# Two transformer blocks in one kernel: joining steps of the third attention

## The reference

```
# 8 heads of 64 in 2 key groups; 512 queries
kc, vc = compress(k_c), compress(v_c)            # 31 compressed keys
s_c = q . kc * scale;  p_c = softmax(s_c masked) * valid_c
o_c = p_c . vc
s_s = q . k_blocks[selected]                     # 8 of at most 8 blocks of 64: all past keys
o_s = softmax(s_s masked) . v_blocks
s_w = q . k_band                                 # a causal window of 256 keys
o_w = softmax(s_w masked) . v_band
g = sigmoid(g_logit)                             # three gates per head
o = g[0] * o_c + g[1] * o_s + g[2] * o_w
```

## Time and profile before

| what | value |
|---|---|
| median of 3 runs | 2524.85 us (2523.75 to 2526.11) |
| the profiled execution | 2522.84 us, its span 2521.0 us |
| granted TensorE clock in it | 1.00 |
| PE, DVE, ACT busy in the span | 99%, 55%, 37% |
| third attention, first scores to the next stage's first product | 1964.16 to 2090.23 us |

### The profile page before, as it was taken

The page is one execution under the profiler, slowest core; times in us unless marked ns, Lnnn a source line. Parts: engine busy times, 40 slices in busy tenths (PEclk is TensorE's granted clock), DMA queues, the critical chain, the costliest instruction groups (busy, mean ns, idle before and its releaser), DMA issues.

```text
span 2521.0 us, 30069 instructions
## 1 busy us (share of the span) xinstructions
PE 2501.9 (99%) x11841; PEld 2023.9 (80%) x11841; DVE 1395.2 (55%) x1962; ACT 943.7 (37%) x1379; POOL 60.4 (2%) x77
## 2 busy tenths in 40 slices
PE   9999999999999999999999999999999999999999
PEld 7788888888888877888888888888777658888887
DVE  6556366645556655555663444566654676733433
ACT  5432334322334444223442232445544574422222
POOL 6000000000000000000001000000000001000000
PEclk9999999999999999999999999999999999999999
DMA  4222223444443311222343333222222111222222
GB/s 164 67 84 96 88 101 104 150 147 150 150 136 115 104 68 69 99 101 84 109 139 126 134 115 133 95 91 101 101 93 75 51 34 67 101 100 100 94 90 100
DMA packets 38629, 260.04 MB, mean 103 GB/s; under 512 B 4417, under 2 KB 4673, under 8 KB 8049
## 3 DMA queue, kind: packets, MB, share of 16 engines
q1 hardware_dynamic: 32976, 226.92, 26.2%
q10 hardware_dynamic: 5296, 30.20, 3.4%
q0 software_dynamic: 240, 1.28, 0.2%
HBM read 256.29 MB, written 2.10 MB: 102 GB/s over the span
## 4 chain that ended last, share of the span: by engine, by line
PE 94%; DVE 4%; ACT 1%; issue 1%; DMA 0%; SPq 0%; DVEq 0%; ACTq 0%
PE ps L2010 65%; PE ps L2037 9%; PE ps L2241 6%; PE ps L2063 5%; PE ps L2184 2%; PE ps L2225 2%; PE ps L2205 1%; PE ps L2467 1%; DVE w_lo L1139 1%; PE ps L2483 1%; PE ps L2163 0%; DVE a_lo L1263 0%; PE ps L2523 0%; PE ps L2329 0%; DVE T L1258 0%
## 5 line engine op out<-in xcount | busy, mean ns | idle before, releaser
L1139 DVE TENSOR_TENSOR w_lo<-raw,w_hi 128x2048 fp32r<-128x2048 f32 x208 | 477.5, 2295 | 325.1 <-ACT w_hi L570 275.3
L2010 PE MATMUL ps<-a_hi,w_hi 128*128 128x512 f32 x1408 | 550.4, 391 | 0.5 <-DVE w_lo L1139 0.3
L2010 PE MATMUL ps<-a_hi,w_lo 128*128 128x512 f32 x1408 | 547.9, 389 | 0.0
L2010 PE MATMUL ps<-a_lo,w_hi 128*128 128x512 f32 x1408 | 547.8, 389 | 0.0
L570 ACT ACTIVATE w_hi<-raw 128x2048 fp32r<-128x2048 f32 x198 | 376.4, 1901 | 404.0 <-PE ps L2010 338.2
L2010 PEld LDWEIGHTS ps<-a_hi,w_hi 128*128 128x128 f32 x1408 | 264.3, 188 | 57.2 <-issue 1.1
L2010 PEld LDWEIGHTS ps<-a_lo,w_hi 128*128 128x128 f32 x1408 | 264.4, 188 | 55.4 <-issue 1.0
L2010 PEld LDWEIGHTS ps<-a_hi,w_lo 128*128 128x128 f32 x1408 | 264.3, 188 | 54.8
L2010 PE MATMUL ps<-f_hi,w_hi 128*128 128x512 f32 x708 | 275.4, 389 | 0.0
L2010 PE MATMUL ps<-f_lo,w_hi 128*128 128x512 f32 x708 | 275.4, 389 | 0.0
L2010 PE MATMUL ps<-f_hi,w_lo 128*128 128x512 f32 x708 | 275.4, 389 | 0.0
(11 more groups left out here) (384 smaller groups left out, 3559.8 us busy)
## 6 DMA issues: line engine op xcount, KB each, us to landing
raw<-weights SPq DMA_DIRECT2D x209, 1024.0 KB, 4.9
ada_w<-ada ACTq DMA_DIRECT2D x24, 1024.0 KB, 4.9
merged<-cmp_w SPq DMA_DIRECT2D x2, 1024.0 KB, 5.8
out<-h SPq DMA_DIRECT2D x8, 256.0 KB, 2.0
h<-x_t SPq DMA_DIRECT2D x3, 512.0 KB, 7.1
raw<-weights SPq DMA_DIRECT2D x4, 256.0 KB, 5.1
kt<-c_row ACTq DMA_DIRECT2D x2, 512.0 KB, 3.6
pads<-p_t ACTq DMA_DIRECT2D x2, 512.0 KB, 4.0
```

The lines of the kernel that those rows point to most:

```text
L1139: dve.tensor_tensor(w_lo[n % 2][:, w], raw[n % 2][:, w], w_hi[n % 2][:, w].bitcast(F32), ALU.subtract)\
L2010: ins = pe.matmul(dst, a[i], b[j], start=done == 0, stop=done == total - 1)
```

## The change

1. In query blocks 0 and 1 the selected and the window step become one step with `parts=2`: one score matmul per head over both key sets (the key operand `kt[r, 0:2, 0:w]` has two stretches), one mask addition and one maximum for four rows of sums, four exponentials, four weighings, and one list of value products. The list has 28 steps instead of 36.
2. A compressed step is done for both heads at once: three DVE instructions before the exponential, one exponential, four DVE instructions after it.
3. PE's value products wait in a list `due` and are issued for two steps at a time (alone at the end of a tile, if they are due there). The transposed probabilities get a third pair of buffers (`qx`), and ACT's copies wait for the products of step s-3 instead of s-2.
4. The maxima, sums and scales of this attention get columns of their own in `small`, which grows from 28 to 60.
5. The table that deals out the 48 gate pieces is a new one.

The lists of the first two kinds of attention and all other stages are as before.

```diff
@@ nsa_steps
+                    if b < 2:
+                        out.append(dict(
+                            w=2 * w, parts=2, masks=((w - P, C("causal")),),
+                            gate=[gt[:, b, 3 * hd + 1:3 * hd + 3] for hd in heads],
+                            sets=[(qt[r, t, b * P:(b + 1) * P], kt[r, 0:2, 0:w]) for r in half],
+                            values=[selected[g] + window[g] for g in range(2)],
...
@@ pieces
-                share = [0] + [2, 2, 1, 1, 2, 1, 1, 1, 1] * 3 + [2, 2, 2, 2, 1, 1, 1, 1]
+                share = [0] + [3, 2, 2, 1, 1, 1, 2] * 3 + [3, 3, 2, 2, 1, 1]
@@ buffers of the transposed probabilities
+            return (pT[0], pT[1], T[2], T[3], qx[:, 2, :], qx[:, 3, :])[2 * (s % 3) + j]
+        def kept(which):
+            return 3 if which > DEPTH else 2
@@ ACT
+                    if x["kind"] == "cmp":
+                        act.activation(both_probs(s), both_scores(s)[:, :, 0:P], ACT.Exp).then_inc(sem("exp_done"), 2)
+                        return
+                    n, w = parts(x)
                     for j in range(2):
+                        m = 2 * s + j
+                        for a in range(n):
+                            at, k, t = slice(a * w, (a + 1) * w), maximum_at(which, s) + n * j + a, total_at(which, s) + n * j + a
+                            ins = act.activation(probs(which, m)[:, at], score_bank(m)[:, at], ACT.Exp,
+                                                 bias=small[:, k:k + 1], scale=1.0, accum_out=small[:, t:t + 1])
+                        ins.then_inc(sem("exp_done"), 1)
...
@@ DVE, maxes
+                        both, top = both_scores(s)[:, :, 0:P], small[:, 52:60].rearrange("p (j b) -> p j b", j=2)
+                        seq(dve.tensor_tensor(both, both, C("cmp_mask").unsqueeze(1).to_broadcast([P, 2, P]), ALU.add))
+                        both = both_blocks(both)
+                        seq(dve.tensor_reduce(top, both, AX.X, ALU.max))
...
+                    if parts(x)[0] == 2:
+                        both = both[:, :, 0:w].rearrange("p j (a n) -> p j a n", a=2)
+                        (lo, mask), = x["masks"]
+                        seq(dve.tensor_tensor(both[:, :, :, lo:lo + P], both[:, :, :, lo:lo + P],
+                                              mask.unsqueeze(1).unsqueeze(1).to_broadcast([P, 2, 2, P]), ALU.add))
+                        dve.tensor_reduce(small[:, k:k + 4].rearrange("p (j a) -> p j a", j=2), both, AX.X, ALU.max,
+                                          negate=True).then_inc(sem("max_made"), 1)
+                        return
...
@@ PE, attention
-                    if s >= 1:
-                        apply(s - 1)
-                apply(len(steps) - 1)
+                    if s >= 1 and steps[s - 1]["kind"] != "cmp":
+                        due.append(s - 1)
+                    if len(due) == 2 or due and (not ahead or steps[due[0]]["closes"]):
+                        for i in due:
+                            apply(i)
+                        due = []
+                for i in due + [len(steps) - 1]:
+                    apply(i)
```

More of the change, by code:

```diff
@@ L321, in nsa_steps @@
                     n = w - k0 * P
[L322 to L337, removed]
+                    base = dict(out=[ps[7][r, b * P:(b + 1) * P] for r in half], tile=t, kind="pair", first=False)
@@ new lines, in nsa_steps @@
+                    selected = [[vt[:, j, 64 * g:64 * g + 64] for j in range(b + 1)] for g in range(2)]
+                    window = [[vt[:, j, P + 64 * g:P + 64 * g + 64] for j in range(k0, b + 1)] for g in range(2)]
+                    if b < 2:
[4 more added lines that the diff above has]
+                            values=[selected[g] + window[g] for g in range(2)],
+                            cmp=[(ps[7][half[g], :], kt[0:CMP_W, 2, 256 + 64 * g:256 + 64 * g + 64], turned_cmp(t, g))
+                                 for g in range(2) if b == 0],
+                            last=False, opens=b == 0, closes=False, **base))
+                    else:
+                        out.append(dict(
+                            w=w, masks=((w - P, C("causal")),),
+                            gate=[gt[:, b, 3 * hd + 1:3 * hd + 2] for hd in heads],
+                            sets=[(qt[r, t, b * P:(b + 1) * P], kt[r, 0, 0:w]) for r in half],
+                            values=selected, last=False, opens=False, closes=False, **base))
+                        out.append(dict(
+                            w=n, masks=((n - P, C("causal")), (0, C("far"))),
+                            gate=[gt[:, b, 3 * hd + 2:3 * hd + 3] for hd in heads],
+                            sets=[(qt[r, t, b * P:(b + 1) * P], kt[r, 1, k0 * P:w]) for r in half],
+                            values=window, last=b == QB - 1, opens=False, closes=b == QB - 1, **base))
@@ L681, in weigh @@
                         return
-                    p = probs(which, 2 * s + 1)[:, 0:steps[s]["w"]]
+                    n, w = parts(steps[s])
                     act.wait_ge(*c.next("scale_made"))
-                    act.activation(p, p, ACT.Copy, scale=small[:, 14 + s % 2:15 + s % 2])\
-                        .then_inc(sem("second_weighed"), 1)
+                    for a in range(n):
+                        p, k = probs(which, 2 * s + 1)[:, a * w:(a + 1) * w], scale_at(s) + a
+                        ins = act.activation(p, p, ACT.Copy, scale=small[:, k:k + 1])
+                    ins.then_inc(sem("second_weighed"), 1)
                 exps(0)
@@ L1355, in weigh @@
                     seq(dve.reciprocal(small[:, 12:14], small[:, 4 + k:6 + k]))
[L1356 to L1359, removed]
+                    for j in range(2):
                         p = probs(which, 2 * s + j)[:, 0:w]
                         weighed = c.next("att_made")
[L1362 to L1366, removed]
+                        dve.tensor_scalar(p, p, small[:, 12 + j:13 + j], None, ALU.mult).then_inc(sem("att_made"), 1)
                 plan = pieces(which)
@@ L2192, in turn @@
                         pe.wait_ge(sem("pT_made"), TURNS[which] + i - in_turn + 1)
-                    pe.wait_ge(*c.next("second_weighed" if j == 1 and "gate" in x else "att_made"))
+                    if j == 0 or x["kind"] != "cmp":
+                        pe.wait_ge(*c.next("second_weighed" if j == 1 and "gate" in x else "att_made"))
                     if which == DEPTH and i == 0:
```

97 lines of the change are left out of this document (52 added, 45 removed).

## The result

The changed kernel takes 2528.67 us (median of 20 runs) where the kernel before takes 2524.31 (20 runs): ratio 1.0016, 95% interval 1.001 to 1.0023, or 4 us more. Two of the 20 runs of the changed kernel took 3574 and 4198 us at a mean granted clock of 0.65 and 0.56; they are slow runs, and the ratio is one of fast runs. The forecast was 2527.2 with "no change that a measurement can tell" as its likeliest class; the time lies in the range (2519.5 to 2531.5).

The account below looks back on a forecast made before the run. PE was taken as the bound; work -6.1, boundary waits +10.5 and other waits -2.0 gave +2.4 us with rounding, thus 2525.2 from the profiled 2522.84 and 2527.2 from the median shown; range 2519.5 to 2531.5 us.

Parts of the forecast that it names:

- PE is the bound, in and behind the stretch: Third attention, first scores to next stage's first product, 126.0 us: PE limits it and what follows, so changes reach the end.
- 6.1 us less work on PE: PE in the third attention: joined score pairs save 1.7, fewer value groups 2.85, fewer groups of gate pieces 1.5 us.
- Five boundary waits, 10.5 us: Between gate tiles sharing one PSUM bank, PE waits for ACT's read: 3.8, 1.9, 1.8, 1.5 and 1.5 us.
- step 23: Fifth tile boundary, inside this step: ACT's weighing starts at 3.87, its read frees PE at 6.18; PE waits 3.8 us.
- Other waits 3.3: PE's waits in the stretch beside the boundaries: 3.3 us instead of 5.3, the largest 0.9 at step 1.
- the walk: Forward count of the PE, DVE and ACT queues with traced durations; 126.6 us for the old order (measured 126.0).
- Unknown prices: Costs absent from the trace: joined mask addition 0.73 us, joined scores 0.64 or 1.06, exponential over both compressed heads 0.43.
- D: Rival on joined scores: two key stretches cost as two groups, 1.7 us comes back, 2529.0 us; chance 0.10.
- B: Rival: DVE between scores and transpose of the eight joined steps becomes the slow link, up to 2531.8 us; chance 0.12.
- C: Rival: PE's saving on group costs isn't there, +6.8 us, with the scores too +8.4, 2533.3 us; chance 0.05.
- sum: work, boundaries, other waits: Total for the third attention: work -6.1, boundaries +10.5, other waits -2.0, giving +2.4 us with rounding.
- Rival A: At the gate tile boundaries ACT reads before PE asks for the bank: -5.1 us, 2519.8 us; chance 0.15.

Follow-up runs that it names:

- e1: The changed kernel with another table for the 48 gate pieces, moving the tile boundaries and gathering the pieces in 17 groups instead of 27: 2512.5 us.
- e2: The changed kernel, table unchanged, with ACT reading a finished gate tile before the exponentials of step s+2 instead of after them: 2521.36 us.
- e8: The changed kernel with the table of e1 and value products issued one step at a time: 2516.63 us.
- e9: The kernel before with nothing but another table for the 48 gate pieces: 2520.66 us.
- e10: The changed kernel without the joined steps, with a table made for that; joint compressed steps and paired products stay: 2516.36 us.
- e11: The kernel before with only the compressed steps for both heads at once and the third pair of buffers added; old table, single products: 2522.64 us.
- e7: The changed kernel with value products issued one step at a time, its table kept: 2528.28 us.
- e3: The changed kernel with idle matmuls (2, 6, 5, 2 and 13) before PE's wait for the bank at the five tile boundaries: 2532.8 us.
- e4: The changed kernel with two pieces of the last tile moved from step 23 to step 24, so only the fifth boundary stands elsewhere: 2525.51 us.
- e6: The changed kernel with 13 idle matmuls only at the fifth tile boundary: 2527.52 us.
- e5: The changed kernel without the joined steps and with the old table; paired products and joint compressed steps stay: 2528.71 us.

## Why the prediction was right, and where it was off

- **PE is the bound, in and behind the stretch.** Right: the stretch grew 5.0 us, the span 4.9.
- **6.1 us less work on PE.** Right, by PE's busy time: 6.0 us less in the changed kernel, once the 3.2 that the lower clock added are taken off. e1's busy time is 7.7 less than before (121.36 to 113.64), where 6.1 and its ten groups of pieces fewer, 1.9, make 8.0.
- **Five boundary waits, 10.5 us.** Right in place, order and releaser. The trace shows 9.2 idle (3.5, 1.7, 1.6, 1.2, 1.1 for the forecast's 3.8, 1.9, 1.8, 1.5, 1.5). The gap is at least in part how it is counted: a wait in brackets starts at the modelled end of a matmul, my 3.8 at the moment the queue was free. By starts alone step 23 was met to 0.02 us.
- **Other waits 3.3.** The trace has 3.3: 0.96 before the transposes of step 1 (0.9 forecast) and seven smaller. In the kernel before they were 4.7 by the trace, 5.3 by the walk.
- **Unknown prices.** Mask addition and joined scores cost what was taken, so D falls, and B: PE's longest wait for probabilities is 0.96. C falls with the two value groups at 1.46 us, with the busy time, and with e1.
- **The term that is missing: the clock.** The step "sum: work, boundaries, other waits" counts a wait at its own length. Two of them cost 1.6 us each beyond that. The stretch grew 5.0 where 2.4 was forecast, 2.6 more: the 3.2 of the clock, less 0.7 by which the net growth of the waits was counted too high (8.5 forecast, 7.8 measured). So the range held although a cost was missing, helped a little by a second error of the other sign. I had read that the clock is at 1.00 in all of the earlier trace rows and took this for given. Rows 2 could not show it, as the old order has no wait over 1.04 us there.
- **The class.** The forecast gave "slower by over 0.2%" 0.14 and "the same" 0.78; the ratio 1.0016 (1.001 to 1.0023) is a small slowdown that is clear of noise; its median lies just inside 0.2%, its interval reaches past it. That "the same" came true says little for the mechanism; the rows of step 23 say more.
- Rival A (the waits are covered) didn't come: all five waits are in the trace. No run takes away these waits and nothing else, so its 2519.8 stays unmeasured; e2, with 3.2 of the 9.2 us left, took 2521.4, and e1, with the boundaries moved and fewer groups, 2512.5.

## What to carry to other kernels

When work is joined or moved, look at what stood between a producer's last piece and the next user of its buffer: here the saved work was real to a few tenths of a microsecond, and a table of numbers that nobody would call a wait gave it back through a single PSUM bank. Walk the queues forward with traced durations for the new order, then choose the table by that walk; it met the stretches of the five variants in which the clock never fell there (e1, e8, e9, e10, e11) within 1.2 us, those of e1 and e8 within 0.1. When comparing tables, count their groups of pieces too, not only their waits. And look at the granted clock behind each wait of TensorE: here two waits of 1.6 and 3.5 us cost 1.6 us each beyond their own length.

## What the runs showed of the hardware that I had not expected

The granted clock fell to 1.2 GHz behind short waits of an engine that was otherwise 90% busy. In the traces of this stretch it fell at or behind every wait of 1.9 us and more: 3.5 us (the changed kernel, e7), 2.4 (e2), 1.9, 2.1 and 2.0 (e3). At waits of 1.6 to 1.7 it was divided: it fell behind one of 1.6 in the changed kernel but not behind the same wait in e4 or e6, behind 1.7 in e4, e5 and e6 but not in the changed kernel or e7. It never fell behind the waits of 1.1 to 1.3. The Trainium skill, "TensorE: Matmul & The Clock Gate", section "Why this matters for your kernels", warns of idle gaps between bursts of matmuls; the trace agrees that gaps bring the clock down, but here shorter gaps than the page names did it too (1.6 to 2.4 us). The clock stayed low for 3.4 us each time, but for 10.2 us in e7, at the same 3.5 us wait that had 3.4 in the changed kernel. What decides between these cases was not tried.
